# Channel mixing of a pooling branch: one four-byte product against three products of rounded and remainder parts

## The chip, the core and the metric

The kernel runs on one core of a Trainium2 chip. The metric is the device time of one execution in microseconds (us), from three timed executions. One further execution was recorded by the hardware profiler, and all rows in this document come from such recordings. TensorE (PE in the profile, PEld for its weight loads) does the matrix products, VectorE (DVE) and ScalarE (ACT) and GpSimd (POOL) do elementwise work, SyncE (SP) issues the DMAs.

## The reference

The program is two blocks behind each other on a sequence of 1024 positions with 1024 features. What matters here is the pooling branch of the first block. The input is normalised and projected (`w_in`); the first 1024 projected features `pool_x` are cut into four groups of 256 channels, and each group gets a centred window mean minus itself along the sequence, with a window of 2, 4, 8 or 16. Then each group's 256 channels are mixed by a 256 x 256 matrix:

```python
pooled = stack([window_mean_minus_self(ug[:, :, g], w) for g, w in enumerate((2, 4, 8, 16))], axis=2)
mixed = einsum('bsgc,gcd->bsgd', pooled, pool_w).reshape(B, S, D_POOL)
y_pool = mixed * pool_scale * silu(pool_z)
```

`pool_z` is the second 1024 projected features. `y_pool` goes through the output projection together with the other branch (an mLSTM), is added to the input and normalised; the second block follows.

## The kernel before

Everything is kept transposed: features on the 128 partitions, positions along the free axis. A weight matrix is worked through in chunks of 256 columns. Each chunk is loaded to `wraw` by SP, cast by POOL to `whi` (type fp32r, line 610), and the remainder `wlo = wraw - whi` is made by POOL (line 612). The activations exist likewise as `u_hi` and `u_lo`. A product of the projection is then three fp32r products added in PSUM: `u_hi` with `wlo` (line 829), `u_lo` with `whi` (830), `u_hi` with `whi` (831); the helper is `three`. One output tile is 128 features x 512 positions and takes 8 contraction steps, so 24 products; a chunk gives 4 tiles.

The pooling stage is a loop over the four groups g, written out by hand in the same order on every engine; the engines meet only at semaphores.

- TensorE: four tiles of `pool_x` (chunk 2g), four tiles of `pool_z` (chunk 2g + 1), then a wait on `v_px` (pooling sums done) and on the load of the mixing matrix `pw`, then the mixing: four tiles, each from two contraction steps (line 930). The operands `px` and `pw` are plain four-byte floats there. The PSUM banks of the projection (a ring of 4) and of the mixing (another ring of 4) are taken again only once the engine that empties them has said so.
- ScalarE: empties the four `pool_x` tiles into `px` (line 1964) after the mixing of the group before has read it, empties the four `pool_z` tiles through Silu into `sz` (1999), then casts the four mixed tiles `yr` to `yp_hi` (2003).
- VectorE: waits until all four tiles of `px` are there; for each of the two feature tiles m it makes g + 1 shifted sums over 1024 positions in `pta` and `ptb` (1381), corrects both edges (1385, 1386) and writes the window mean minus itself back into `px` (1387), signalling `v_px`. Then it scales and gates the mixed tiles into `yr` (1397, two buffers), and makes `yp_lo = yr - yp_hi` (1405).
- POOL splits the chunks; it is ahead of TensorE by one chunk at most, since a buffer `whi[w % 2]` has to be read out first.
- SP loads `pw` for the groups (436, two buffers) between the chunks, behind a wait on `a_rel`, a small result of the same stretch.

`yp_hi` is a [128, 8, 1024] fp32r tile and `yp_lo` another; group g fills feature tiles 2g and 2g + 1 of them. After the fourth group TensorE goes straight on with the output projection: its first chunk reads feature tiles 0 to 3 and needs half of `yp_lo` (`v_ylo` 8), its second chunk reads tiles 4 to 7 and needs all of it (`v_ylo` 16). Then come the projections, recurrence and second block, which are not touched.

Of the kernel before, what the change touches and what calls it, by code (L numbers as in the profile page):

```python
# [7 lines left out]
F32 = mybir.dt.float32  # L8
F32R = mybir.dt.float32r
ALU = mybir.AluOpType  # L10
ACT = mybir.ActivationFunctionType
AX_X = mybir.AxisListType.X

P = 128
S = 1024
# [3 lines left out]
HALF = 512  # L19
CW = 256  # L20
# [6 lines left out]
PAD = 16  # L27
# [79 lines left out]
def build(nc, I, out):  # L107
# [64 lines left out]
    with ctx:  # L172
# [12 lines left out]
        def sem(name):  # L185
# [22 lines left out]
        xr, yp_hi, um, ym_hi, x2_hi, res = region(  # L208
            SL, [("xr", [P, NT, D], F32)], [("yp_hi", [P, KT, S], F32R)], [("um", [P, KT, S], F32)],
            [("ym_hi", [P, KT, S], F32R)], [("x2_hi", [P, KT, S], F32R)], [("res", [P, NT, D], F32)])  # L210
# [2 lines left out]
            [("ym_lo", [P, KT, S], F32R)], [("x2_lo", [P, KT, S], F32R)], [("y2c", [P, 2, 2, S], F32R)])  # L213
        qTs, kts, vs, STs = (qT0, qT1), (kt0, kt1), (v0, v1), (ST0, ST1)

        xn = Q[:, 0, :].rearrange("p (t c) -> p t c", t=NT)
        cn = Q[:, 3, :].rearrange("p (t c) -> p t c", t=NT)
        gated = [Q[:, q, :].rearrange("p (m s) -> p m s", m=2) for q in range(3)]
# [2 lines left out]
        def y2(j, part):  # L221

            if j < 4:
# [1 line left out]
            return (y2b, y2c)[j // 2 - 2][:, j % 2, part, :]  # L225

        (_k, vrow, vrow2, junk, relst, hot,
         px, pta, ptb, sz, yr, pw,
         hst,
         cva, mzs, bd, bt, wg, ga,  # L230
         hc0, Pm, kwb, bdh, Amat, hc1, Cst, tmpi, yt0, gs, nM, cols,
# [7 lines left out]
            [("_k", [P, 4 * XPAD], F32), ("vrow", [V_CW2, P], F32), ("vrow2", [V_N - V_CW2, P], F32), ("junk", [P, D], F32),  # L239
             ("relst", [8, RELS], F32), ("hot", [33, RELS], F32)],  # L240
            [("px", [P, 2, XPAD], F32), ("pta", [P, XPAD], F32), ("ptb", [P, XPAD], F32),
             ("sz", [P, 2, S], F32), ("yr", [P, 2, HALF], F32), ("pw", [P, 2, 2, CW], F32)],
            [("hst", [P, NT, HALF], F32)],
            [("cva", [P, 2, S], F32), ("mzs", [P, 2, HALF], F32), ("bd", [P, KT, P], F32),
             ("bt", [P, 3, KT, P], F32), ("wg", [P, 24, 2, 8], F32), ("ga", [P, 16, 32], F32)],
# [20 lines left out]
        def brd(q):  # L266
# [29 lines left out]

        names = (

            "l_wraw l_cst l_mask l_hot l_rows l_g l_wn l_gb l_wg l_pw0 l_pw1 l_xh0 l_xh1 l_h0 l_h1 l_h2 l_h3 "
            "l_smz l_sml l_br0 l_br1 l_br2 l_br3 l_am l_ln l_rows2 l_rb0 l_rb1 l_kB l_po "  # L300

            "o_rel o_band o_h0 o_h1 o_mz0 o_mz1 o_sp0 o_sp1 o_out "
# [7 lines left out]
            "v_tot v_h v_hn v_y1 v_h2 v_lnv v_nmr v_xh v_x2lo v_bnv v_ln2 v_ug v_sp v_yab v_cv2 v_s v_rc "  # L310
            "v_o v_cg v_pT v_y2lo v_r2 v_gain v_out "

            "a_rel a_ss a_sd a_uhi a_px a_sz a_yhi a_um a_c a_mz a_bt a_r a_hq a_st a_W a_tmp a_t1 "
            "a_ymhi a_ss2 a_x2hi a_q a_av a_wsT a_glu a_k a_f a_cs "
            "a_p a_pT a_cg a_y2hi a_vt a_out "

# [2 lines left out]
        s = {n: sem(n) for n in names}  # L319
# [64 lines left out]
        def _(sp_):  # L384
# [42 lines left out]
            sp_.dma_start(sink[:, :], I["attn_sink_2"][0].partition_broadcast(P)).then_inc(s["l_gb"], 16)  # L427
            wt(1)

            sp_.wait_ge(s["a_rel"], 1)  # L430
            sp_.dma_start(row_t.ap(), relst[:, :]).then_inc(s["o_rel"], 16)

            for g in range(4):
                if g >= 2:
                    sp_.wait_ge(s["t_mix"], 4 * (g - 1))
                sp_.dma_start(pw[:, g % 2, :, :], I["pool_w"][0, g].rearrange("(k p) n -> p k n", p=P)
                              ).then_inc(s[f"l_pw{g % 2}"], 16)
                for w in (2 * g + 2, 2 * g + 3):
                    wt(w)
                if g == 0:  # L440
                    sp_.wait_ge(s["o_rel"], 16)
                    sp_.dma_start(rel_d, bass.AP(row_t, 0, [[RELS, 8], [0, P], [1, RELS]])).then_inc(s["o_band"], 16)
# [360 lines left out]
        def _(pe):  # L803
# [17 lines left out]
            def ring_x(name, value):  # L821
                b = 4 + ring[1] % 4
                ring[1] += 1
                return take(b, name, value)
# [84 lines left out]
            for g in range(4):  # L909
                for i in range(0 if g else 3, 4):  # L910
                    group(2 * g, i, u_hi, u_lo, "a_px", 4 * g + i + 1)
                if g == 0:

                    pe.wait_ge(s["l_rows"], 16 * 11)
                    ps = ring_x("v_vec", 2)
                    pe.transpose(ps[:, 0:V_CW2], vrow[:, :], cst[0:V_CW2, C_ID:C_ID + V_CW2])
                    pe.transpose(ps[:, V_CW2:V_N], vrow2[:, :], cst[0:V_N - V_CW2, C_ID:C_ID + V_N - V_CW2]
                                 ).then_inc(s["t_vec"], 1)
                    pe.wait_ge(s["l_hot"], 32)
                    ps = ring_x("a_rel", 1)  # L920
                    pe.matmul(ps[0:8, :], relw[:, :], hot[:, :], start=True, stop=True).then_inc(s["t_vec"], 1)
                for i in range(4):
                    group(2 * g + 1, i, u_hi, u_lo, "a_sz", 4 * g + i + 1)
                pe.wait_ge(s["v_px"], 2 * g + 2)
                pe.wait_ge(s[f"l_pw{g % 2}"], 16 * (g // 2 + 1))
                for i in range(4):
                    dt, nh = i // 2, i % 2
                    ps = ring_x("v_yr", 4 * g + i + 1)
                    for k in range(2):
                        mm = pe.matmul(ps[:, :], pw[:, g % 2, k, dt * P:(dt + 1) * P],  # L930
                                       px[:, k, PAD + nh * HALF:PAD + (nh + 1) * HALF],
                                       start=(k == 0), stop=(k == 1))
                    mm.then_inc(s["t_mix"], 1)
            pool_hi = lambda j: yp_hi[:, j, :]
            pool_lo = lambda j: yp_lo[:, j, :]
# [386 lines left out]
        def _(ve):  # L1322
# [46 lines left out]
            ve.wait_ge(s["g_init"], 5)  # L1369
            k = 0  # L1370
            for g in range(4):
                ve.wait_ge(s["a_px"], 4 * g + 4)
                w = WINDOWS[g]
                left = (w - 1) // 2
                for m in range(2):
                    src, width = px[:, m, :], XPAD
                    for step in range(g + 1):
                        dst = (pta, ptb)[step % 2]
                        sh = 1 << step
                        width -= sh  # L1380
                        chain(ve.tensor_tensor(dst[:, 0:width], src[:, 0:width], src[:, sh:sh + width], ALU.add))
                        src = dst
                    tot = src[:, PAD - left:PAD - left + S]
                    e = C_EDGE + 16 * g
                    chain(ve.tensor_tensor(tot[:, 0:8], tot[:, 0:8], cst[:, e:e + 8], ALU.mult))
                    chain(ve.tensor_tensor(tot[:, S - 8:S], tot[:, S - 8:S], cst[:, e + 8:e + 16], ALU.mult))
                    ve.scalar_tensor_tensor(px[:, m, PAD:PAD + S], tot, 1.0 / w, px[:, m, PAD:PAD + S],
                                            ALU.mult, ALU.subtract).then_inc(s["v_px"], 1)
                    ve.wait_ge(s["v_px"], 2 * g + m + 1)
                ve.wait_ge(s["a_sz"], 4 * g + 4)  # L1390
                for i in range(5):
                    if i < 4:
                        n = 4 * g + i
                        dt, nh = i // 2, i % 2
                        ps = filled(ve, "t_mix", n + 1, "v_yr", n + 1)
                        ve.wait_ge(s["a_yhi"], max(n - 1, 1)) if n >= 2 else None
                        ve.scalar_tensor_tensor(yr[:, n % 2, :], ps[:, :], VT[:, V_PS + 2 * g + dt:V_PS + 2 * g + dt + 1],
                                                sz[:, dt, nh * HALF:(nh + 1) * HALF], ALU.mult, ALU.mult
                                                ).then_inc(s["v_yr"], 1)
                    if i:  # L1400
                        n = 4 * g + i - 1
                        dt, nh = (i - 1) // 2, (i - 1) % 2
                        sl = slice(nh * HALF, (nh + 1) * HALF)
                        ve.wait_ge(s["a_yhi"], n + 1)
                        ve.tensor_tensor(yp_lo[:, 2 * g + dt, sl], yr[:, n % 2, :],
                                         yp_hi[:, 2 * g + dt, sl].bitcast(F32), ALU.subtract
                                         ).then_inc(s["v_ylo"], 1)
                        ve.wait_ge(s["v_ylo"], n + 1)
# [525 lines left out]
        def _(ac):  # L1934
# [49 lines left out]
            for g in range(4):  # L1984
                if g:
                    ac.wait_ge(s["t_mix"], 4 * g)
                for i in range(0 if g else 2, 4):
                    pooled(g, i)
                if g == 0:

                    ps = filled(ac, "t_vec", 3, "a_rel", 1)
                    ac.activation(relst[:, :], ps[0:8, :], ACT.Copy).then_inc(s["a_rel"], 1)
                    ac.wait_ge(s["o_rel"], 16)
                else:
                    ac.wait_ge(s["v_yr"], 4 * g)
                for i in range(4):
                    m, nh = i // 2, i % 2
                    ps = filled(ac, "t_gemm", first[2 * g + 1] + i + 1, "a_sz", 4 * g + i + 1)
                    ac.activation(sz[:, m, nh * HALF:(nh + 1) * HALF], ps[:, :], ACT.Silu).then_inc(s["a_sz"], 1)
                for i in range(4):  # L2000
                    n = 4 * g + i
                    ac.wait_ge(s["v_yr"], n + 1)
                    ac.activation(yp_hi[:, 2 * g + i // 2, (i % 2) * HALF:(i % 2 + 1) * HALF], yr[:, n % 2, :],
                                  ACT.Copy).then_inc(s["a_yhi"], 1)
# [384 lines left out]
```

## Time and profile before

| what | us |
|---|---|
| median of 3 timed runs | 1254.55 (1253.87 to 1254.64) |
| the profiled execution | 1250.48 |
| its span, first to last instruction | 1248.6 |
| TensorE busy (matmuls) | 1208.9 (97%) |
| VectorE busy | 660.4 (53%) |
| GpSimd busy | 469.4 (38%) |
| ScalarE busy | 349.6 (28%) |
| time of the four groups of the pooling stage, start of the profile's clock | about 16 to 226 |

The profiled execution is 4.1 us, or 0.3%, under the median of the timed ones. Matmuls overlap each other in the records (each is shown with some 390 ns, though the next starts 227 ns later), so that their pace is read from the starts, or from the chain that ended last, which gives each piece only the time that it adds.

### The profile page before, as it was taken

Reading aid. Unit: us, or ns where it says so; the run is one execution under the profiler, and the core shown is the slowest. Engines: PE = TensorE matmul, PEld = TensorE weight load, DVE = VectorE, ACT = ScalarE, POOL = GpSimd, SP = SyncE. Lnnn points to the kernel's source line nnn. Section 1 sums busy time; section 2 is a strip of 40 time slices with the busy share of each in tenths; the row PEclk is TensorE's granted clock in tenths of the full one; section 3 lists DMA queues with packets and bytes.
Section 4 is the critical chain, followed back from the end, with each engine's and each line's share of the span. In section 5 each row is a group of like instructions: output and inputs, shape, how many; then the busy total and the mean of one; then the engine's idle time right before and its main releaser. Section 6 shows DMA issues by size and latency. Waiting matters only on the chain.

```text
span 1248.6 us, 15984 instructions
## 1 busy us (share of the span) xinstructions
PE 1208.9 (97%) x5977; PEld 966.7 (77%) x5977; DVE 660.4 (53%) x1220; ACT 349.6 (28%) x710; POOL 469.4 (38%) x449
## 2 busy tenths in 40 slices
PE   6999999999999999999998999889999999999995
PEld 5777878788888878787786788779888886667784
DVE  4325355422465203167767946856694525445468
ACT  6211110100022112446565421321111144433211
POOL 3224222232545223444665654314322324443343
PEclk9999999999999999999999999989999999999998
DMA  6131121243311223100114412222121110051112
GB/s 216 56 131 43 36 75 34 101 169 101 75 49 53 68 68 106 60 26 24 54 39 144 166 46 70 83 97 69 51 68 35 59 35 35 5 190 34 37 50 118
DMA packets 72702, 92.84 MB, mean 74 GB/s; under 512 B 12721, under 2 KB 51849, under 8 KB 72114
## 3 DMA queue, kind: packets, MB, share of 16 engines
q1 hardware_dynamic: 63906, 87.62, 21.0%
q10 hardware_dynamic: 8720, 4.20, 1.2%
q8 instruction: 49, 0.80, 0.3%
q14 instruction: 27, 0.22, 0.1%
HBM read 74.45 MB, written 18.92 MB: 75 GB/s over the span
## 4 chain that ended last, share of the span: by engine, by line
PE 88%; DVE 6%; POOL 2%; DMA 1%; issue 1%; ACT 1%; SPq 0%; ACTq 0%; POOLq 0%; DVEq 0%
PE bank L829 22%; PE bank L831 21%; PE bank L830 21%; PE bank L1078 3%; PE bank L1095 3%; PE wide L1251 2%; PE wide L930 2%; PE bank L1232 2%; PE wide L1241 2%; PE wide L1088 2%; DVE res L1908 1%; DMA wraw<-in_w_in 1%; PE bank L1038 1%; PE bank L1049 1%; PE bank L1026 1%
## 5 line engine op out<-in xcount | busy, mean ns | idle before, releaser
L610 POOL CAST whi<-wraw 128x2048 fp32r<-128x2048 f32 x32 | 60.6, 1894 | 448.9 <-PE bank L831 361.1
L829 PE MATMUL bank<-u_hi,wlo 128*128 128x512 f32 x512 | 202.7, 396 | 2.9 <-DVE u_lo L1349 2.9
L831 PE MATMUL bank<-u_hi,whi 128*128 128x512 f32 x512 | 200.1, 391 | 0.0
L830 PE MATMUL bank<-u_lo,whi 128*128 128x512 f32 x512 | 199.9, 390 | 0.0
L612 POOL TENSOR_TENSOR wlo<-wraw,whi 128x2048 fp32r<-128x2048 f32 x33 | 155.9, 4725 | 3.1 <-ACT whi L2230 0.5
L829 PE MATMUL bank<-x_hi,wlo 128*128 128x512 f32 x320 | 129.2, 404 | 7.2 <-POOL wlo L612 6.4
L830 PE MATMUL bank<-x_lo,whi 128*128 128x512 f32 x320 | 125.5, 392 | 0.0
L831 PE MATMUL bank<-x_hi,whi 128*128 128x512 f32 x320 | 125.5, 392 | 0.0
L829 PEld LDWEIGHTS bank<-u_hi,wlo 128*128 128x128 f32 x512 | 96.6, 189 | 25.9 <-DVE u_lo L1349 4.0
L831 PEld LDWEIGHTS bank<-u_hi,whi 128*128 128x128 f32 x512 | 96.5, 188 | 20.4
L830 PEld LDWEIGHTS bank<-u_lo,whi 128*128 128x128 f32 x512 | 96.5, 188 | 20.2 <-issue 0.7
L829 PEld LDWEIGHTS bank<-x_hi,wlo 128*128 128x128 f32 x320 | 60.6, 189 | 28.8 <-issue 9.8
L775 POOL TENSOR_SCALAR sp<-sp,rcx 128x384 f32<-128x384 f32 (+1 forms) x64 | 36.0, 575 | 112.3 <-DVE rcx L1840 112.3
L831 PEld LDWEIGHTS bank<-x_hi,whi 128*128 128x128 f32 x320 | 60.6, 189 | 13.1
L830 PEld LDWEIGHTS bank<-x_lo,whi 128*128 128x128 f32 x320 | 60.7, 190 | 11.6
L1753 DVE SCALAR_TENSOR_TENSOR wide<-glu,VT,wide 128x1024 f32<-128x1024 f32 x58 | 69.3, 1283 | 0.0
L1095 PE MATMUL bank<-v,kwb 128*128 128x257 f32 x224 | 58.2, 383 | 1.1 <-DVE Cst L1556 0.9
L1078 PE MATMUL bank<-Cst,qT 128*128 128x257 f32 x224 | 58.1, 381 | 0.9 <-ACT tmpj L2149 0.8
L2020 ACT ACTIVATE um<-bank 128x512 f32<-128x512 f32 x16 | 9.6, 599 | 157.2 <-PE bank L831 157.2
L698 POOL TENSOR_TENSOR Pm<-ST,Wb 128x128 f32<-128x128 f32 x64 | 30.4, 475 | 59.0 <-ACT Wb L2101 59.0
L829 PE MATMUL bank<-whi,ym_lo 128*128 128x512 f32 x128 | 50.2, 392 | 0.2 <-ACT tmpj L2149 0.2
L1834 DVE CUSTOM_DVE_ANT_0 sp<-bank,rbias,nsink 128x384 f32<-128x384 f32 (+1 forms) x64 | 34.9, 583 | 29.4 <-PE bank L1232 29.1
(330 smaller groups left out, 2430.7 us busy)
## 6 DMA issues: line engine op xcount, KB each, us to landing
wraw<-in_w_in SPq DMA_DIRECT2D x27, 1024.0 KB, 5.4
wraw<-in_w_out SPq DMA_DIRECT2D x12, 1024.0 KB, 5.1
xr<-in_x SPq DMA_DIRECT2D x8, 512.0 KB, 8.7
hst<-in_x SPq DMA_DIRECT2D x4, 1024.0 KB, 6.0
hpool<-hst SPq DMA_DIRECT2D x4, 1024.0 KB, 4.1
smz<-mzs SPq DMA_DIRECT2D x16, 256.0 KB, 2.1
wraw<-nmax ACTq DMA_DIRECT2D x32, 128.0 KB, 3.0
h<-hpool SPq DMA_DIRECT2D x4, 1024.0 KB, 6.8
```

What stands on the lines that cost most here:

```text
L610: g_.tensor_copy(whi[w % 2][:, :, :], wraw[:, :, :]).then_inc(s["w_hi"], 1)
L612: g_.tensor_tensor(wlo[w % 2][:, :, :], wraw[:, :, :], whi[w % 2][:, :, :].bitcast(F32), ALU.subtract).then_inc(s["w_lo"], 1)
L698: g_.tensor_tensor(Pm[:, n % 2, :], STs[h % 2][:, ck, :], Wb[:, n % 2, :], ALU.mult).then_inc(s["g_P"], 1)
L775: g_.tensor_scalar(row, row, rcx[:, x % 2, i:i + 1], 0.5 if g else 1.0, ALU.mult, ALU.mult).then_inc(s["g_nm"], 1)
L829: pe.matmul(ps, al, bh, start=(k == 0), stop=False)
L830: pe.matmul(ps, ah, bl, start=False, stop=False)
L831: return pe.matmul(ps, ah, bh, start=False, stop=(k == nk - 1))
L930: mm = pe.matmul(ps[:, :], pw[:, g % 2, k, dt * P:(dt + 1) * P], px[:, k, PAD + nh * HALF:PAD + (nh + 1) * HALF], start=(k == 0), stop=(k ...
L1078: mm = pe.matmul(ps[:, 0:AUG], q[:, k, ck * P:(ck + 1) * P], Cst[:, d, k, :], start=(k == 0), stop=(k == 1))
L1095: mm = pe.matmul(ps[:, 0:AUG], kwb[:, m % 2, k * P:(k + 1) * P], v[:, ck, :], start=True, stop=True)
L1753: ins = ve.scalar_tensor_tensor(dst, src, w, acc, ALU.mult, ALU.add)
L1834: ve.tensor_tensor_reduce(sp[:, x % 2, i, BAND - nb * P:BAND], ps[:, 0:nb * P], rbias[:, 2 * p + i, off:off + nb * P], 1.0, nsink[:, h:h + 1],
```

## The change

- TensorE's mixing (line 930) is no longer one product of four-byte `pw` and `px` for each of the two contraction steps, but `three` of the parts `pwhi`, `pwlo` and `pxhi`, `pxlo`, all fp32r.
- ScalarE makes `pwhi` (one cast of 128 x 512 numbers, ahead of the Silu tiles) and `pxhi` (two casts of 128 x 1024, one behind each of the first two Silu tiles, each behind a wait for that feature tile's pooling).
- VectorE makes `pwlo` (one subtraction of 128 x 512) and `pxlo` (two of 128 x 1024) behind the pooling. `v_px` now counts five steps for each group, and TensorE waits for the fifth.
- `pxhi` and `pxlo` lie in feature tiles 6 and 7 of `yp_hi` and `yp_lo`. These are group 3's own output, so in group 3 ScalarE waits for the end of the mixing (`t_mix` 16) before it writes `yp_hi`.
- VectorE's wait for `px` is now per feature tile: the sums of tile m start when its two halves are there (in group 0 when all four are, since that group's tiles come in another order).
- `pw` has one buffer. Its first load is issued ahead of the wait on `a_rel`; the later ones wait for `pwlo` of the group before, not for the mixing.

```diff
+        pxhi, pxlo = yp_hi[:, 6:8, :], yp_lo[:, 6:8, :]
...
-             ("sz", [P, 2, S], F32), ("yr", [P, 2, HALF], F32), ("pw", [P, 2, 2, CW], F32)],
+             ("sz", [P, 2, S], F32), ("yr", [P, 2, HALF], F32), ("pw", [P, 2, CW], F32),
+             ("pwhi", [P, 2, CW], F32R), ("pwlo", [P, 2, CW], F32R)],
...  SyncE
+            mix_weights(0)
             sp_.wait_ge(s["a_rel"], 1)
...
             for g in range(4):
-                if g >= 2:
-                    sp_.wait_ge(s["t_mix"], 4 * (g - 1))
-                sp_.dma_start(pw[:, g % 2, :, :], ...).then_inc(s[f"l_pw{g % 2}"], 16)
+                if g:
+                    sp_.wait_ge(s["v_px"], 5 * g - 2)
+                    mix_weights(g)
...  TensorE
-                pe.wait_ge(s["v_px"], 2 * g + 2)
-                pe.wait_ge(s[f"l_pw{g % 2}"], 16 * (g // 2 + 1))
+                pe.wait_ge(s["v_px"], 5 * g + 5)
                 for i in range(4):
                     dt, nh = i // 2, i % 2
                     ps = ring_x("v_yr", 4 * g + i + 1)
+                    c, t = slice(dt * P, (dt + 1) * P), slice(nh * HALF, (nh + 1) * HALF)
                     for k in range(2):
-                        mm = pe.matmul(ps[:, :], pw[:, g % 2, k, dt * P:(dt + 1) * P],
-                                       px[:, k, PAD + nh * HALF:PAD + (nh + 1) * HALF],
-                                       start=(k == 0), stop=(k == 1))
+                        mm = three(ps[:, :], ((pwhi[:, k, c], pwlo[:, k, c]), (pxhi[:, k, t], pxlo[:, k, t])), k, 2)
...  VectorE
             for g in range(4):
-                ve.wait_ge(s["a_px"], 4 * g + 4)
...
                 for m in range(2):
+                    ve.wait_ge(s["a_px"], 4 * g + 2 * m + 2 if g else 4)
...
-                    ve.wait_ge(s["v_px"], 2 * g + m + 1)
+                    ve.wait_ge(s["v_px"], 5 * g + m + 1)
+                ve.wait_ge(s["a_mixhi"], 3 * g + 1)
+                ve.tensor_tensor(pwlo[:, :, :], pw[:, :, :], pwhi[:, :, :].bitcast(F32), ALU.subtract
+                                 ).then_inc(s["v_px"], 1)
+                for m in range(2):
+                    ve.wait_ge(s["a_mixhi"], 3 * g + m + 2)
+                    ve.tensor_tensor(pxlo[:, m, :], px[:, m, PAD:PAD + S], pxhi[:, m, :].bitcast(F32), ALU.subtract
+                                     ).then_inc(s["v_px"], 1)
...  ScalarE
+                ac.wait_ge(s["l_pw"], 16 * (g + 1))
+                ac.activation(pwhi[:, :, :], pw[:, :, :], ACT.Copy).then_inc(s["a_mixhi"], 1)
                 for i in range(4):
...
                     ac.activation(sz[:, m, nh * HALF:(nh + 1) * HALF], ps[:, :], ACT.Silu).then_inc(s["a_sz"], 1)
+                    if i < 2:
+                        ac.wait_ge(s["v_px"], 5 * g + i + 1)
+                        ac.activation(pxhi[:, i, :], px[:, i, PAD:PAD + S], ACT.Copy).then_inc(s["a_mixhi"], 1)
+                if g == 3:
+                    ac.wait_ge(s["t_mix"], 16)
```

## Rows read from the trace of the kernel before

**Rows 1.** The page: span, TensorE's share, and the chain that ended last.

```profile
span 1248.6 us, 15984 instructions
...
PE 1208.9 (97%) x5977; PEld 966.7 (77%) x5977; DVE 660.4 (53%) x1220; ACT 349.6 (28%) x710; POOL 469.4 (38%) x449
...
PE 88%; DVE 6%; POOL 2%; DMA 1%; issue 1%; ACT 1%; SPq 0%; ACTq 0%; POOLq 0%; DVEq 0%
```

**Rows 2.** Chain that ended last, in order of time: start us, us added, what.

```profile
67.79 0.23 PE bank L831
68.02 6.87 PE wide L930 x16
74.88 0.24 PE bank L829
...
118.47 6.87 PE wide L930 x16
...
219.36 6.87 PE wide L930 x16
226.22 0.24 PE bank L829
```

**Rows 3.** Line 930 alone: count, duration ns (min/median/max), starts, shapes.

```profile
L930 PE MATMUL wide<-px,pw x64: 590/592/592, 67.9 to 225.6; 128*128 128x512 f32 x64
```

**Rows 4.** Stretches: span, then PE, PEld, DVE, ACT, POOL busy, granted clock, DMA.

```profile
16.00:19.50 3.50, 3.41 (x9) 2.72 (x10) 3.50 (x6) 3.50 (x7) 3.50 (x3) 0.56 0.88 143
...
74.90:118.40 43.50, 43.50 (x193) 35.95 (x193) 17.27 (x16) 5.45 (x9) 7.39 (x2) 1.00 0.18 57
118.40:125.40 7.00, 7.00 (x18) 3.13 (x17) 4.21 (x3) 1.86 (x3) 6.41 (x2) 1.00 0.00 0
```

**Rows 5.** Chain in order of time at the very start of the projection.

```profile
16.98 0.43 PE bank L831
```

**Rows 6.** VectorE in time: start, us, line, operation, tiles, [idle before, releaser].

```profile
50.34 1.23 DVE L1387 SCALAR_TENSOR_TENSOR px<-pta,px 128x1024 f32<-128x1024 f32 x1
...
198.34 2.40 DVE L1381 TENSOR_TENSOR pta<-px 128x1055 f32<-128x1055 f32 x1 [18.61 <-ACT px L1964]
200.78 5.54 DVE L1381 TENSOR_TENSOR ptb<-pta 128x1053 f32<-128x1053 f32 x1
...
210.58 1.26 DVE L1381 TENSOR_TENSOR pta<-px 128x1055 f32<-128x1055 f32 x1
...
216.14 1.23 DVE L1387 SCALAR_TENSOR_TENSOR px<-ptb,px 128x1024 f32<-128x1024 f32 x1
221.29 0.75 DVE L1397 SCALAR_TENSOR_TENSOR yr<-wide,VT,sz 128x512 f32<-128x512 f32 x1 [3.92 <-PE wide L930]
...
223.50 3.04 DVE L1405 TENSOR_TENSOR yp_lo<-yr,yp_hi 128x512 fp32r<-128x512 f32 x1
...
229.48 0.69 DVE L1405 TENSOR_TENSOR yp_lo<-yr,yp_hi 128x512 fp32r<-128x512 f32 x1 [0.17 <-ACT yp_hi L2003]
```

**Rows 7.** ScalarE in order of time, group 0's second Silu tile, then group 3.

```profile
57.17 0.60 ACT L1999 ACTIVATE sz<-bank 128x512 f32<-128x512 f32 x1 [3.50 <-PE bank L831]
...
186.75 0.60 ACT L1964 ACTIVATE px<-bank 128x512 f32<-128x512 f32 x1 [4.78 <-PE bank L831]
...
203.13 0.60 ACT L1999 ACTIVATE sz<-bank 128x512 f32<-128x512 f32 x1 [4.90 <-PE bank L831]
208.51 0.60 ACT L1999 ACTIVATE sz<-bank 128x512 f32<-128x512 f32 x1 [4.78 <-PE bank L831]
...
222.08 0.63 ACT L2003 ACTIVATE yp_hi<-yr 128x512 fp32r<-128x512 f32 x1 [2.08 <-DVE yr L1397]
```

**Rows 8.** POOL in order of time, group 3: the splits of two chunks.

```profile
199.71 5.49 POOL L612 TENSOR_TENSOR wlo<-wraw,whi 128x2048 fp32r<-128x2048 f32 x1
219.50 1.89 POOL L610 CAST whi<-wraw 128x2048 fp32r<-128x2048 f32 x1 [14.29 <-PE bank L831]
221.47 4.53 POOL L612 TENSOR_TENSOR wlo<-wraw,whi 128x2048 fp32r<-128x2048 f32 x1
```

**Rows 9.** The queue of SP in order of time: start, us of issue.

```profile
46.99 0.38 SPq L436 DMA_DIRECT2D pw<-in_pool_w x1
47.42 12.63 SPq L394 DMA_DIRECT2D wraw<-in_w_in x2
```

More of the change, by code:

```diff
@@ L227, in build @@
         (_k, vrow, vrow2, junk, relst, hot,
-         px, pta, ptb, sz, yr, pw,
+         px, pta, ptb, sz, yr, pw, pwhi, pwlo,
          hst,
@@ L297, in build @@
         names = (
-            "l_wraw l_cst l_mask l_hot l_rows l_g l_wn l_gb l_wg l_pw0 l_pw1 l_xh0 l_xh1 l_h0 l_h1 l_h2 l_h3 "
+            "l_wraw l_cst l_mask l_hot l_rows l_g l_wn l_gb l_wg l_pw l_xh0 l_xh1 l_h0 l_h1 l_h2 l_h3 "
             "l_smz l_sml l_br0 l_br1 l_br2 l_br3 l_am l_ln l_rows2 l_rb0 l_rb1 l_kB l_po "
@@ L311, in build @@
             "v_o v_cg v_pT v_y2lo v_r2 v_gain v_out "
-            "a_rel a_ss a_sd a_uhi a_px a_sz a_yhi a_um a_c a_mz a_bt a_r a_hq a_st a_W a_tmp a_t1 "
+            "a_rel a_ss a_sd a_uhi a_px a_mixhi a_sz a_yhi a_um a_c a_mz a_bt a_r a_hq a_st a_W a_tmp a_t1 "
             "a_ymhi a_ss2 a_x2hi a_q a_av a_wsT a_glu a_k a_f a_cs "
@@ L428, in _, with mix_weights @@
             wt(1)
+            def mix_weights(g):
+                sp_.dma_start(pw[:, :, :], I["pool_w"][0, g].rearrange("(k p) n -> p k n", p=P)
+                              ).then_inc(s["l_pw"], 16)
+            mix_weights(0)
             sp_.wait_ge(s["a_rel"], 1)
@@ L433, in _ @@
             for g in range(4):
-                if g >= 2:
-                    sp_.wait_ge(s["t_mix"], 4 * (g - 1))
-                sp_.dma_start(pw[:, g % 2, :, :], I["pool_w"][0, g].rearrange("(k p) n -> p k n", p=P)
-                              ).then_inc(s[f"l_pw{g % 2}"], 16)
+                if g:
+                    sp_.wait_ge(s["v_px"], 5 * g - 2)
+                    mix_weights(g)
                 for w in (2 * g + 2, 2 * g + 3):
```

## The prediction

> **What bounds the kernel now.** I read three views, from coarse to fine. The page first: TensorE is busy for 97% of the span, and the chain that ended last is 88% TensorE [rows 1]. The chain in order of time says where in the pooling stage that holds: it runs from projection tile to mixing block to projection tile on TensorE without another engine between, in all four groups. The reader is to see that the start of each row is the start of the one before plus its time (67.79 + 0.23 = 68.02, 68.02 + 6.87 = 74.89) [rows 2]. So TensorE waits for nobody here, and what is taken from its queue comes off the end, unless an operand is late or a later stage keeps it. Last, VectorE, ScalarE and POOL in order of time: how long before the end of the Silu tiles (E below) their results are there.
>
> **TensorE's mixing.** It removes 8 four-byte products a group (4 tiles x 2 steps). The trace has 64 records for these 32 products, thus 16 a group [rows 3], and a group takes 6.87 us: 6.87 / 16 = 0.43 us a record, 0.86 us a product [rows 2]. It adds 8 x 3 = 24 fp32r products. Their pace is read from the projection between two mixings: 8 tiles x 24 = 192 products from 74.88 to 118.47, so 43.59 / 192 = 0.227 us each [rows 2]; the first one behind a mixing took 0.24 us. [...] 24 x 0.227 = 5.45 us. A group saves 6.87 - 5.45 = 1.42 us, four groups 5.7 us. Bounds on the new product: 0.227 us from below, as no fp32r row of this size is faster; from above 0.24 us (5.76 us a group, a gain of 1.11, in all 4.4 us). At the low clock a product took 0.43 us [rows 5] with 0.56 granted [rows 4]; that is how TensorE starts after it stood idle, and it is taken up under the rivals. I take 0.227, since the new products have the shape and types of the projection's.
>
> [...]
>
> **Are the new operands in time?** This is the only new wait of TensorE: it used to wait for the pooling, now for three subtractions more on VectorE, which in turn wait for ScalarE's casts. Group 3 has the longest pooling (four sums), so I work it through; E = 219.36 [rows 2].
> - Feature tile 0 now starts when its second half is emptied, 186.75 + 0.60 = 187.35 [rows 7]. Undisturbed the pooling of a tile takes 217.37 - 210.58 = 6.8 us [rows 6]. So it is done by 194.2, before the cast and subtraction of POOL that lie around 199.71 [rows 8].
> - Feature tile 1 must wait for the fourth half, which was the old start, 198.34. It then meets what tile 0 met: a sum of 2.40 and one of 5.54 us instead of 1.26 [rows 6], beside POOL's subtraction [rows 8]. Tile 0 took from 198.34 to 210.58 in that place, so tile 1 is done at 210.6 instead of 217.4.
> - `pwlo` is 512 numbers a partition: 0.69 us by the last `yp_lo` row [rows 6], to 211.3. Its `pwhi` is a ScalarE cast of 0.63 us [rows 7] between 198.3 and 203.13, where ScalarE is idle.
> - `pxlo` of tile 0, 1024 numbers: 1.26 us by a sum of that length [rows 6], to 212.6. Its `pxhi` follows the Silu tile of 203.13 and takes 2 x 0.63 = 1.26 us [rows 7]: ready at 205.0.
> - `pxhi` of tile 1 follows the Silu tile of 208.51 and must wait for 210.6: ready at 211.9. `pxlo` of tile 1 ends at 213.9.
>
> That leaves 219.4 - 213.9 = 5.5 us of cover. Groups 1 and 2 have one or two sums fewer for each tile, so more cover. Group 0 is another case, as its tiles don't start early: pooling is done at 50.34 + 1.23 = 51.6 [rows 6], but `pxhi` of tile 1 stands behind the Silu tile of 57.17 and ends at 57.17 + 0.60 + 1.26 = 59.0 [rows 7]. `pxlo` of tile 1 follows by 61 even if the one before it is held up by POOL for as long as the 3.04 us row [rows 6]; E is 68.02 [rows 2], so 7 us are left. The new work of VectorE (0.69 + 2 x 1.26 = 3.2 us a group) and ScalarE (0.63 + 2 x 1.26 = 3.2 us) thus costs nothing.
>
> **What is queued behind ScalarE's new waits.** Behind the wait for the pooling of tile 1 stands the third Silu tile, which comes 5.4 us after the second; the wait and cast end at 211.9, before that. If they didn't, nobody would notice for long: TensorE needs that bank again only for the next group's tile. Price: none.
>
> **Group 3's wait for the end of mixing.** `yp_hi` started at 222.08, 2.7 us after E [rows 7]; now it starts at E + 5.45. The first `yp_lo` took 3.04 us and ended at 226.5, E + 7.2 [rows 6], because it stood beside POOL's subtraction (221.47 to 226.0) [rows 8]. Now it starts at about E + 6.2 and ends there too, at E + 7.2. So the last `yp_lo` stays near E + 11 (229.48 + 0.69 - 219.36 = 10.8); as bound from above, each of the four steps runs serially behind the mixing, E + 5.45 + 4 x (0.63 + 0.75 + 0.69) = E + 13.7. Needed is it by the second chunk of the output projection, at E + 5.45 + 192/2 x 0.227 = E + 27.2, and by the loads of the residual input into `hst`, whose first use has the eight free banks as cover. Price: none; 13 us of cover.
>
> **SP and the loads of `pw`.** The first load moves ahead of a wait, from 46.99 to the time when the chunk before it is issued; the next chunk load stood right behind it, at 47.42, and gains 0.4 us that nobody waits for [rows 9]. Later loads wait for `pwlo` of the group before, which is earlier than the next chunk load can be issued, so nothing behind them moves. Both ways the price is zero: TensorE waits for none of it.
>
> **Does the gain reach the end?** 12% of the chain isn't TensorE [rows 1], and all of it lies behind the pooling stage. But each stretch there begins at something that TensorE delivered, so it starts 5.7 us earlier as well; nothing in the stage runs by a clock of its own. I take the whole 5.7, and the bound is that all is lost (a gain of 0).
>
> **Sum.** For the profiled execution 1250.48 - 5.7 = 1244.8. The median of the runs shown is 4.1 us above that execution; the sum is a difference, so on that scale it is 1254.55 - 5.7 = 1248.9 us.
>
> **Rivals.**
> - *A, the gain is given back behind the stage.* A stretch set by another engine starts by something that did not move. For it: 12% of the chain is off TensorE. Against: no start outside of TensorE's order is in sight. It gives up to 1254.5; a chance of 6%.
> - *B, new products at another price.* With 0.24 us each the gain is 4.4, so 1250.1. [...] Chance 20% together; the sign doesn't change. The point from which it would be a loss is 6.87 / 24 = 0.286 us a product.
> - *C, slower: the remainders come late.* A VectorE operation with two inputs in SBUF that meets a POOL subtraction is held until that ends: 5.54 us instead of 1.26 [rows 6] beside the 5.49 us one [rows 8]. If each of the three new subtractions were held like that, they would take 16.6 instead of 3.2 us, and group 3's operands would be there at 213.9 + 13.4 = 227.3, 7.9 us past E; groups 0 to 2, with about 7 us of cover, some 6 us late each. That is +26 - 5.7 = +20 us: 1275. Also TensorE would have stood idle and might start again at 0.43 us a product. It decides from 5.5 us of delay in group 3. Against it: POOL is idle from 205.2 to 219.50 (14.29 us in its row) [rows 8], and the new subtractions lie at 210.6 to 213.9. Chance 4%.
> - *D, it doesn't do what it says*: the early start of the sums saves nothing by itself, as TensorE never waited for them; that is in the sum already. That the mixing still runs as four-byte products would give 1254.5; 1%.
>
> [...]
>
> **How the numbers follow.** The sum as it stands holds 69%, B 20%, A 6%, C 4%, D 1%. The range reaches from 1246.3 (the 6.9 us gain, and 1.4 us for the place of a median) to 1252.5 (the 4.4 us gain, half of what A could take, and the same doubt of the median). What a measurement of this kernel can tell from no change is about 0.2%, 2.5 us: the sum and B lie beyond it, most of A and D within it. So faster 0.90, same 0.06, slower 0.04.
>
> **What the profile after would show.** Mixing blocks of 24 products with about 5.45 us each in the chain, and the next projection row starting right behind. The last `pxlo` of group 3 ends about 5.5 us before its mixing starts, and TensorE has no wait named for it. Pooling of tile 0 in groups 1 to 3 starts at about the second `px` tile, and the sums of tile 1 carry the long rows. The last `yp_lo` lies near E + 11. A wait of TensorE on `pxlo`, a product over 0.24 us, or a stretch behind 226 us that is longer than before would make the prediction wrong.

## The result, and the profile after

| | before | changed |
|---|---|---|
| median of the timed executions, us | 1254.21 (1252.36 to 1254.64, 4) | 1243.94 (1242.91 to 1246.59, 4) |
| ratio to before | | 0.9924 [0.9905, 0.9944] |
| the profiled execution, us | 1250.48 | 1246.59 |
| its span, us | 1248.6 | 1244.8 |

The changed kernel is faster, as forecast, but the median lies 10.3 us under the one before, not 5.7, and under the low end of the range (1246.3). The two profiled executions differ by only 3.9 us. So 5.7 was wrong by either pair, in opposite directions, and the question is where the rest comes from. One execution of the changed kernel in the second repeat below took 1361.8 us at a granted clock of 0.845; it stands far off all others and is in none of the numbers that follow but one median, 1245.08, which is 1245.06 without it.

The changed kernel's chain in order of time, first and fourth mixing block (start us, us added, what; answers to [rows 2]):

```profile
67.50 0.23 PE bank L837
67.73 0.23 PE wide L835
...
72.94 0.23 PE wide L837
73.17 0.23 PE bank L835
...
214.38 0.23 PE bank L837
214.61 0.23 PE wide L835
...
219.82 0.23 PE wide L837
220.05 0.23 PE bank L835
```

The mixing block is the run of "wide" rows between two "bank" rows: 73.17 - 67.73 = 5.44 us, and 220.05 - 214.61 = 5.44 us in group 3, where the kernel before had 6.87 [rows 2]. Four times 1.43 is 5.7 us. Nobody is waited for between.

VectorE and ScalarE of the changed kernel in time, group 3 (answers to [rows 6, 7]):

```profile
182.71 1.26 DVE L1385 TENSOR_TENSOR pta<-px 128x1055 f32<-128x1055 f32 x1 [6.15 <-ACT px L1975]
...
193.59 2.40 DVE L1385 TENSOR_TENSOR pta<-px 128x1055 f32<-128x1055 f32 x1 [4.09 <-ACT px L1975]
196.03 5.55 DVE L1385 TENSOR_TENSOR ptb<-pta 128x1053 f32<-128x1053 f32 x1
...
205.85 0.69 DVE L1395 TENSOR_TENSOR pwlo<-pw,pwhi 128x512 fp32r<-128x512 f32 x1
206.46 2.35 DVE L1399 TENSOR_TENSOR yp_lo<-px,yp_hi 128x1024 fp32r<-128x1024 f32 x2
...
224.82 0.69 DVE L1416 TENSOR_TENSOR yp_lo<-yr,yp_hi 128x512 fp32r<-128x512 f32 x1 [0.17 <-ACT yp_hi L2021]
```

```profile
205.85 1.06 ACT L2015 ACTIVATE yp_hi<-px 128x1024 fp32r<-128x1024 f32 x1 [1.48 <-DVE px L1391]
...
220.09 1.15 ACT L2021 ACTIVATE yp_hi<-yr 128x512 fp32r<-128x512 f32 x2 [4.84 <-PE wide L837]
```

The sums of tile 0 start beside the projection, 11 us before those of tile 1, and the long sums (2.40 and 5.55 us) have moved to tile 1. The last remainder ends at 206.46 + 2.35 = 208.8, 5.8 us before the mixing starts. The last `yp_lo` of the stage ends at 225.5, 10.9 us behind the Silu products.

What the forecast had not looked at is TensorE's clock behind the stage. Stretches in which it is granted at 0.50 (columns as in [rows 4]), first of the kernel before, then of the changed one:

```profile
419.21:422.62 3.41, 3.41 (x18) 3.41 (x17) 0.00 (x0) 0.98 (x2) 0.00 (x0) 0.50 0.00 0
811.74:818.56 6.82, 4.59 (x11) 3.62 (x12) 6.61 (x9) 1.31 (x2) 3.32 (x4) 0.50 0.19 77
```

```profile
411.99:418.81 6.82, 6.82 (x29) 6.47 (x29) 0.00 (x0) 1.58 (x3) 0.00 (x0) 0.50 0.01 2
807.94:814.76 6.82, 4.61 (x11) 3.64 (x12) 6.61 (x9) 1.32 (x2) 3.31 (x4) 0.50 0.20 79
```

At the same place of the program (the small products of the gates) the profiled execution before was halved for 3.4 us and the one after for 6.8 us. The chains show it, too, before (first fence) and after:

```profile
414.02 3.48 PE wide L967 x32
417.50 1.79 PE wide L970 x16
```

```profile
407.70 3.48 PE wide L971 x32
411.18 2.56 PE wide L974 x16
```

Up to the first of these rows the changed kernel is 414.02 - 407.70 = 6.3 us ahead: 5.7 from the mixing, 0.3 from the first chunk, which landed sooner in that execution (9.18 instead of 9.49 us), the rest unnamed. The second row of the pair, the same 16 products, takes 1.79 before and 2.56 after. At a granted 0.50 a product takes 0.43 us in the changed kernel's chain (417.34), at 1.00 0.23 (419.00), so by estimate one more halved stretch of 3.41 us costs half of its length, 1.7 us, if TensorE works through all of it; that leaves 4.6 us. The lead at the end is 3.8 us: another 0.25 us goes in the wait behind 800 us (6.66 instead of 6.41 us), the rest of the 0.8 in small pieces that I can't name. A single execution thus carries some microseconds that belong to it and not to the kernel, and so may a median of three or four.

### The profile page after: what moved, and what is told of

Same layout as the page of the kernel before. It is cut to its first block, busy times and chain, and to the rows that moved or that the text cites. A ratio compares the mean times of both kernels' runs of the same rounds, so it can differ in the third digit from the quotient of the medians.

```text
span 1244.8 us, 16078 instructions
## 1 busy us (share of the span) xinstructions
PE 1204.7 (97%) x6009; PEld 973.9 (78%) x6009; DVE 675.2 (54%) x1232; ACT 359.8 (29%) x722; POOL 471.1 (38%) x449
## 4 chain that ended last, share of the span: by engine, by line
PE 88%; DVE 6%; POOL 2%; issue 1%; DMA 1%; ACT 1%; SPq 0%; ACTq 0%; POOLq 0%; DVEq 0%
PE bank L835 22%; PE bank L836 21%; PE bank L837 21%; PE bank L1082 4%; PE bank L1099 3%; PE wide L1255 2%; PE bank L1236 2%; PE wide L1245 2%; PE wide L1092 2%; DVE res L1919 1%; DMA wraw<-in_w_in 1%; PE bank L1053 1%; PE bank L1042 1%; PE wide L836 1%; PE wide L837 1%
## 5 line engine op out<-in xcount | busy, mean ns | idle before, releaser
L835 PEld LDWEIGHTS bank<-x_hi,wlo 128*128 128x128 f32 x320 | 60.6, 189 | 29.1 <-issue 9.8
L837 PEld LDWEIGHTS bank<-x_hi,whi 128*128 128x128 f32 x320 | 60.6, 189 | 13.1
```

The source lines that it names most:

```text
L835: pe.matmul(ps, al, bh, start=(k == 0), stop=False)
L837: return pe.matmul(ps, ah, bh, start=False, stop=(k == nk - 1))
```

## The experiments

Two explanations stand against each other. T: each execution is a fixed time plus 1.7 us for each 3.4 us of halved clock, their number changes from execution to execution, and the kernels differ by 5.7. U: the change saves more than the mixing, in a place that the profiles don't show.

**The changed kernel again**, on another occasion, without an edit.

> The changed kernel once more, against the kernel before on the same chip. The two profiles have the mixing blocks 5.66 us shorter in all, but the profiled executions differ by 3.9 us and the medians by 10.3 us. Theory T (half-clock slots): each execution is a fixed time plus 1.7 us for each slot of 3.4 us in which TensorE's clock is granted at half, and the number of slots changes from execution to execution; then the spans of either kernel differ by steps of about 1.7 us, the granted clock falls with them, and executions with as many slots differ by 5.7 to 6.3 us. Rival U (a second saving in the change that the profile does not show): the spans of equal granted clock differ by 8 us or more.

Measured: 1245.47 us (median of 5) against 1251.33 (23 executions of the kernel before, 1248.41 to 1255.25), ratio 0.9946 [0.9931, 0.9961]. And a third time:

> The changed kernel a third time, for more executions. Theory T: spans between 1241 and 1246, on average 6 us under the kernel before (5.7 of the mixing, the rest from the count of half-clock slots).

Measured: 1245.08 against 1251.04 (11 executions), ratio 0.9949 [0.9934, 0.9963]. So the two repeats differ from before by 5.9 and 6.0 us, and the first comparison was the odd one. With those taken beside the kernels with fillers (below) there are 50 executions of the kernel before: mean 1251.6, median 1251.5, from 1248.4 to 1255.3. They come from two chips, 23 and 27 executions, with means of 1251.5 and 1251.7, so the chip doesn't make the difference between these; which chip had the first comparison isn't on record. Only 5 of the 50 are as slow as the three that the forecast was anchored on (1253.87 and above). Put in order of the granted clock, mean spans in us of the 50 and of the 14 executions of the changed kernel (number of executions in brackets; 15 of the 50, at 0.988 and 0.985, have no partner and are left out):

| granted clock | before | changed | difference |
|---|---|---|---|
| 0.992 | 1247.1 (7) | 1241.2 (2) | 5.9 |
| 0.991 | 1248.9 (6) | 1243.4 (3) | 5.5 |
| 0.990 | 1248.3 (8) | 1242.8 (5) | 5.5 |
| 0.989 | 1249.9 (10) | 1244.8 (3) | 5.1 |
| 0.987 | 1252.1 (4) | 1245.8 (1) | 6.3 |

At equal clock the kernels differ by 5 to 6 us, and either kernel moves by 5 us between the first and the last line. U asked for 8 us or more and falls. The executions don't stand in clean steps of 1.7 us, as T had put it; a halved stretch costs less where TensorE waits in part of it (4.59 of 6.82 us busy in the row at 811.74).

**Everything but the products, and the early sums alone.**

```diff
-                        mm = three(ps[:, :], ((pwhi[:, k, c], pwlo[:, k, c]), (pxhi[:, k, t], pxlo[:, k, t])), k, 2)
+                        mm = pe.matmul(ps[:, :], pw[:, k, c], px[:, k, PAD + nh * HALF:PAD + (nh + 1) * HALF],
+                                       start=(k == 0), stop=(k == 1))
```

> All casts, subtractions, early sums and waits of the change, but the mixing stays one four-byte product for each step (pw then waits for the mixing before it is loaded again). Theory T: the new work of ScalarE and VectorE is hidden, so 0 against the kernel before, within 1.7 us (one slot). Rival U: some 4 us faster, what the median gained over the 5.7. If the preparation cost something it would be slower.

Measured: 1250.87 (12 executions) against 1251.33, ratio 0.9999 [0.9986, 1.0012]. (The edit also makes SP wait for the mixing before it loads `pw` again.) The casts, subtractions and waits cost nothing that this interval shows, and the profile agrees: TensorE waits for nobody between 40 and 240 us, and with the same three halved stretches as the kernel before (3.4, 3.4 and 6.8 us) the span is 1248.4 against 1248.6 us. The other one is the kernel before with the wait on `a_px` moved into the loop over m:

> The kernel before with VectorE's wait for px per feature tile and nothing else. Theory T: 0 (within 0.2%, or one slot of 1.7 us), TensorE never waited for the sums. Rival U with the early sums as its cause: some 4 us faster.

Measured: 1252.05 (10) against 1251.33, ratio 0.9997 [0.9986, 1.0009]. Neither part of the change saves anything by itself; what it brings is in the products.

**Fewer products.**

```diff
-                        mm = three(ps[:, :], ((pwhi[:, k, c], pwlo[:, k, c]), (pxhi[:, k, t], pxlo[:, k, t])), k, 2)
+                        mm = pe.matmul(ps[:, :], pwhi[:, k, c], pxhi[:, k, t], start=(k == 0), stop=(k == 1))
```

> Leaves out the two products with remainders in the mixing: one fp32r product of the rounded parts for each step, 8 instead of 24 a group. Theory: TensorE sets the pace, so 64 products of 0.227 us go, 14.5 us less than the changed kernel, 20.2 us less than the kernel before (about 1234), unless the slots of low clock change in number, 1.7 us each. A mixing block then takes 1.8 us in the chain.

Measured: 1233.42 (4 executions, 1230.8 to 1236.5), ratio 0.9849 [0.9829, 0.9869]. Its first mixing block in the chain:

```profile
66.03 1.81 PE wide L936 x8
67.84 0.23 PE bank L835
```

1.81 instead of 5.44 us, thus 3.63 a group and 14.5 in all, as expected. The medians say only 12.1 (1245.47 - 1233.42). At a granted 0.991 the spans are 1229.0 (a single execution) and 1243.4, which is 14.4 apart, but that this meets the 14.5 is in part chance. Up to the wait behind 785 us the profile is 16.2 us ahead of that of the second repeat, 14.5 for the products and 1.7 for one halved stretch of 3.4 us fewer. Then comes a loss: the chunk load ahead of the wait took 7.64 us (5.97 in the run `fill` below), the wait is longer than in the other kernels (8.24 us), and 10.24 us of halved clock begin in it instead of 6.83 (the load in the chain, then TensorE's product behind the wait):

```profile
778.62 7.64 DMA wraw<-in_w_in
```

```profile
793.79 0.80 PE L835 MATMUL bank<-x_hi,wlo 128*128 128x512 f32 x1 [8.24 <-POOL wlo L618]
```

From a tile of ScalarE before this wait to another behind it (`glu` at 807.60 and 843.18 us in the kernel before) this execution needs 38.0 us, the kernel before 35.6 and the repeats of the changed kernel 35.5 and 35.6. So 2.4 us of a gain were given back there, in this one execution; whether this also happened in the other three isn't known.

**Keeping TensorE busy in a wait.** Behind 800 us TensorE waits for a remainder that POOL makes; in the profiles above the halved clock begins in this wait and reaches past it (811.74 to 818.56 us in the kernel before, the wait until 813.97). In the kernel before:

```profile
807.17 0.39 PE L831 MATMUL bank<-x_hi,whi 128*128 128x512 f32 x1
813.97 0.80 PE L829 MATMUL bank<-x_hi,wlo 128*128 128x512 f32 x1 [6.41 <-POOL wlo L612]
```

The edit, before the first product that needs the remainder (the next product into that bank overwrites what the fillers leave there):

```diff
-                group(W_2 + w, i, x2_hi, x2_lo, "a_glu", n)
+                ps = None
+                if (w, i) == (1, 0):
+                    ps = ring_g("a_glu", n)
+                    for _ in range(27):
+                        pe.matmul(ps[:, :], whi[W_2 % 2][:, 0, 0:P], x2_hi[:, 0, 0:HALF], start=True, stop=True)
+                group(W_2 + w, i, x2_hi, x2_lo, "a_glu", n, ps=ps)
```

> The changed kernel, and in the second block, where TensorE waits 6.3 to 6.7 us for the remainder of a weight chunk (around 803 to 809 us), 27 products of 0.227 us into the bank that is filled next; their result is overwritten. Theory T: the clock was halved for two slots of 3.4 us behind this wait because TensorE stood idle; kept busy it keeps its clock, no slot there, so about 3.4 us less than the changed kernel (9 us less than the kernel before, ratio about 0.993 or less). If the slots come from something else, the time stays or gets longer by what the filler overhangs.

> The changed kernel with the 27 filler products again. Spans from 1240.8 to 1242.4 were found; the same is expected, 8.4 us under the kernel before on average (5.7 from the mixing, 2.7 from the filler).

> The kernel before with the 27 filler products alone. Theory T: about 3.4 us less than the kernel before. Against the run that has the change and the filler it tells once more what the change itself brings: 5.7 us.

> The changed kernel with 9 filler products instead of 27: TensorE still stands idle for about 4.3 us of the 6.5. Theory T: idle time makes the slots, so some come back: 0 to 2 slots behind 808 us, and the mean lies between the changed kernel and the one with 27, 1 to 2.5 us over the latter. If it is the mere presence of a few products that keeps the clock, it equals the one with 27.

| kernel | median us | ratio to before | granted clock of its executions |
|---|---|---|---|
| changed, 27 fillers | 1242.99 | 0.9932 [0.9917, 0.9946] | 0.991 to 0.994 |
| the same again | 1242.71 | 0.9930 [0.9916, 0.9943] | 0.993 to 0.994 |
| changed, 9 fillers | 1246.17 | 0.9953 [0.9938, 0.9968] | 0.989 to 0.993 |
| before, 27 fillers | 1248.43 | 0.9976 [0.9965, 0.9987] | 0.990 to 0.995 |

The stretch behind the wait with 27 fillers (first fence, of the run `fill2`) and with 9 (second fence: in the wait, then the halved stretch, which begins there):

```profile
808.50:815.30 6.80, 6.80 (x31) 5.60 (x31) 6.52 (x12) 2.08 (x3) 0.81 (x1) 1.00 0.24 96
```

```profile
804.00:807.70 3.70, 0.76 (x4) 0.29 (x2) 3.63 (x3) 0.00 (x0) 3.70 (x1) 1.00 0.00 0
807.77:814.59 6.82, 5.40 (x13) 4.29 (x14) 6.58 (x10) 1.49 (x2) 2.51 (x4) 0.50 0.20 79
```

With 27 fillers TensorE goes through at a granted 1.00, in all five profiles of kernels that have them. With 9 it stands idle for 4.4 us up to 809.19, its clock is halved for 6.82 us from 807.77 on, and the gain is gone in the median (3.5 us over the 27 fillers, where 1 to 2.5 was expected; one of its six executions, at 0.993 and 1242.9 us, is as fast as those with 27, and has no profile). So it is the idle time, and not the want of a few products, that goes before this halving. By the medians the fillers are worth 2.4 us in the changed kernel (1245.1 to 1242.7) and 3.4 in the kernel before (1251.85 to 1248.43). In place they are worth the same 2.0 us in both: between the two `glu` tiles of ScalarE named above the kernel before needs 35.6 us, with fillers 33.5; the changed kernel 35.5 to 35.8, with fillers 33.5 and 33.7, and with 9 of them 36.0. That is less than 3.4, since TensorE isn't at work in all of the halved time: half of the 4.6 us that it works there is 2.3. Executions also scatter less: the standard deviation is 0.6 us with fillers (12 executions) against 1.2 without in the changed kernel (10), and 1.3 (11) against 1.8 (50) in the kernel before. That makes this pair the best measure of the change: the means are 1248.9 (11 executions) and 1243.0 (12), 5.9 us apart, with a standard error of 0.4. The profiles of this pair have the same halved time, 6.8 us each before TensorE's last products, and spans of 1246.9 against 1241.1 and 1240.6 us.

**Spreading the small products.** The block at 407 us, where the clock also falls, was cut in three, its parts behind three projection tiles.

> The changed kernel with the block of small products (48 records with 16 columns, 5.3 us, then 16 with 128 columns) at about 407 us cut in three and put behind three projection tiles instead of one. Same work. Theory T: that place has a half-clock slot (1 in the profile before, 2 in the profile after) because TensorE is thinly used there; spread out it has fewer, so 0 to 3.4 us less than the changed kernel. If the slots don't hang on the thin stretch, nothing changes.

> Both edits. Theory T: the gains add up, 3.4 to 6.8 us less than the changed kernel, and executions differ less from each other than those of the kernel before (which spread over 6.8 us, four slots).

Measured: 1246.07, ratio 0.9951 [0.9936, 0.9965], and 1243.08, ratio 0.9926 [0.9909, 0.9943] with single executions from 1239.4 to 1244.9. Against 1245.1 to 1245.5 and 1242.7 to 1243.0 without the spreading nothing is gained, where up to 3.4 and 3.4 to 6.8 us were expected; with both edits executions scatter more, not less (2.1 against 0.6 us). In both profiles the halved time lies at 418 to 420 us instead of 412 and has 3.4 us, and one more stretch of 3.4 us lies at 517 to 519. That one isn't the spreading's: `fill` has one there too, at 517 us. Nor is the 3.4: of the changed kernels without the spreading `fill`, `fill2` and `hi_only` have 3.4 us at the small products, the others 6.8. That the thin stretch at 407 us is what lowers the clock there is not shown; what decides between 3.4 and 6.8 us there stays open.

**Late sums.** What the wait per feature tile is good for: the changed kernel with 27 fillers and the old place of the wait.

```diff
-                    ve.wait_ge(s["a_px"], 4 * g + 2 * m + 2 if g else 4)
+                    ve.wait_ge(s["a_px"], 4 * g + 4)
```

> The changed kernel with the filler, but VectorE waits for all four px tiles before the sums of either feature tile, as in the kernel before. In the trace of the changed kernel group 3 has sums from 182.7 for tile 0 and 193.6 for tile 1 and the Silu products end at 214.6. Both tiles behind 193.6 end at 212.6, then pwlo to 213.3, pxlo of tile 0 to 214.5, pxlo of tile 1 to 215.7: TensorE waits about 1.1 us, in group 3 alone. So 1.1 us more than the changed kernel with the filler, with a wait of TensorE on yp_lo at line 1399. If the early sums don't matter, 0 and no wait.

Measured: 1245.50, ratio 0.9952 [0.9938, 0.9966]. All waits of TensorE between 40 and 240 us (line waited for: us in total, times, longest), then VectorE's last subtraction and the first product of the mixing in the chain:

```profile
PE wide L835 <- DVE yp_lo L1404: 1.1, 1, 1.1
```

```profile
211.93 2.35 DVE L1404 TENSOR_TENSOR yp_lo<-px,yp_hi 128x1024 fp32r<-128x1024 f32 x2
...
214.34 0.50 PE wide L835
```

One wait, in group 3, of 1.1 us, as expected, and the first product behind it takes 0.50 instead of 0.23 us, so 1.4 us in all. The median is 2.8 us over the 27 fillers with early sums, though. At an equal granted clock of 0.994 the spans are 1242.35 (2 executions) and 1240.9 (7), 1.4 us apart; the profiled executions, which have 6.8 us of halved clock each, are 1242.2 against 1241.1 and 1240.6. So the late sums cost about 1.4 us, and the rest of the median goes with a lower clock: two of the six executions were granted 0.990 and 0.991, against one of twelve under 0.992.

## Why the prediction was wrong

- **TensorE's mixing**: right. 5.44 us a block forecast as 5.45; 0.227 us a product against 0.86, so 3.8 to 1. The granted clock is 1.00 in both stretches of the kernel before that the prices come from [rows 4] and in the changed block (67.73 to 73.17), so they compare. The low end of the range, 1246.3, takes a gain of 6.9 us; no run shows that term, the four blocks gain 5.7.
- **Operands in time**: right. The last subtraction ends 5.8 us before the mixing, 5.5 forecast; the two `pxlo` take 2.35 together, the casts 1.06 each instead of 1.26. The casts and subtractions by themselves measured 0.9999 of before. What rival C took for a sum that meets POOL's subtraction, that it is held until that ends, was seen again with one correction: the 5.55 us sum started at 196.03, 1.1 us after the start of POOL's (194.97 to 200.46), and ended at 201.58, 1.1 us behind POOL's end. The 5.54 us one of the kernel before also ended 1.1 us behind POOL's (206.32 against 205.20). None of group 3's new operations met one, but group 0's two `pxlo` did: 2.01 us beside POOL's cast and 2.13 us beside its subtraction, instead of 1.2, and again each ended 1.1 us behind POOL's. So the new VectorE work is 4.8 us in group 0 and not 3.2; the second `pxlo` ended at 60.6, as allowed for (61), 7.1 us before the mixing, and nobody waited.
- **Group 3's wait, SP's queue**: right, at no cost; the last `yp_lo` ends 10.9 us behind the Silu products (10.8 before).
- **Does the gain reach the end?** Right: 6.3 us ahead at 407 us, and 5.9 us (standard error 0.4) between the two kernels with fillers. Rivals A to D did not happen in the changed kernel.
- **The step that failed is the scale**: "so on that scale it is 1254.55 - 5.7 = 1248.9 us", and the "1.4 us for the place of a median" in the range. The profiled execution stood 4.1 us under the three timed ones, and I only noted that. Its own rows granted 0.50 at 419 and 811 us, and I had read the clock at the start alone. Executions of one kernel spread over 7 us, and the slower ones have the lower granted clock. The median of 50 executions of the kernel before is 1251.5, so the three that I took stood 3.1 us over it where the range allowed 1.4; 1251.5 less 5.7 is 1245.8, and the two repeats of the changed kernel have 1245.5 and 1245.1. The measured 10.3 us is made of about 6.2 us between the middles of the two kernels (1251.5 and 1245.3) and 4.1 us by which few executions of either lay off their middle: 1254.21 is 2.7 over, 1243.94 is 1.4 under.
- **What stays open**: why the first three executions before were all that slow. Only 5 of the 50 are, so three of three by mere chance would happen about once in a thousand times. Their granted clock isn't known; that more halved time lay behind them, and not another cause, is inferred from the 50.
- **The clock at the start** was told as how TensorE begins after it stood idle, which the profiles don't show as a rule. It stood idle for 1.2 to 2.8 us before the first projection product in every profile, but 8 of the 14 profiles have 3.4 us of halved clock there and 6 have none. It is one of the terms that change from execution to execution, 1.7 us of the lead.
- **The range's upper end** doesn't follow from its terms: 1254.55 - 4.4 is 1250.15, and with half of what A could take (2.2) and 1.4 for the median that is 1253.7, not 1252.5. The miss was at the other end.

## What to carry to other kernels

A four-byte product took 0.86 us here at 128 x 128 x 512, three fp32r products 0.68; the exchange pays where the two casts and two subtractions fit under other work, and the remainder that comes last must be looked up against the first product that needs it (starting the sums of the first tile early was worth no time before the change and 1.4 us after it, 1.1 of them waiting). Where a profiled execution stands off the timed ones by more than their own spread, look at the granted clock of every stretch before placing a forecast, and make the range as wide as single executions differ, not as three of them do. Where a busy TensorE waits for some microseconds, look at the clock in and behind the wait: the one of 6.3 to 6.7 us here cost more than its length, since 6.8 us of halved clock began in it; filling it with discarded products gave back 2.0 us in place and 2.4 us in the medians of the changed kernel.

## What the runs showed of the hardware that I had not expected

The halved clock came in stretches of 3.4, 6.8 or 10.2 us in the profiles, at the same few places of the program (around 16, 410 to 420, 517 to 525 and 808 us; 14 to 20 us earlier in `hi_only`), but whether one came, and how long it was, changed between executions of one kernel. Besides, in all 14 it was halved for the last 8 to 11 us of the span, beginning 2 to 5 us after TensorE's last product. Behind 800 us each idle time of 6.3 to 6.7 us (7 profiles), and one of 4.4 us, had 6.8 us of halved clock that began in it, 2.5 to 4.9 us after its start, and one of 8.2 us had 10.2, begun 3.9 us after its start; with 0.4 to 0.5 us of waiting there was none. The idle time of 1.2 to 2.8 us before the first projection product had 3.4 us behind it in 8 profiles (1.9 to 2.6 us idle) and none in 6 (1.2 to 2.8 us idle). A 1.7 us difference in a kernel of 1250 us was therefore hidden in single executions (1.8 us standard deviation in the kernel before, 1.2 in the changed one) and came out best with the wait filled (1.3 and 0.6 us).
